# Filler products in TensorE's waits, and the mixer's small products in another order

## What is computed

```python
for l in range(DEPTH):          # 2
    h = rms_norm(x, norm_mix_g) * (1 + sc_m) + sh_m
    proj = h @ w_in             # neighbourhood, latent and grouped-query attention, 3 gates
    x = x + g_m * (merged @ w_out)
    h = rms_norm(x, norm_ffn_g) * (1 + sc_f) + sh_f
    x = x + g_f * ((silu(gate) * up) @ ffn_w_down)
x = rms_norm(x, final_norm_g)
```

```python
h = mixer(x, ...)               # branches y_lru, y_gdn, y_sb, y_gla, gated and merged
x = layer_norm(DN_ALPHA * x + h, ln1_g, ln1_b)
h = moe(x, w_router, router_bias, w_gate, w_up, w_down)
x = layer_norm(DN_ALPHA * x + h, ln2_g, ln2_b)
```

## Time and profile before

| what | value |
|---|---|
| median of 3 runs | 1788.84 us (1787.88 to 1794.1) |
| the profiled execution, its own time | 1784.76 us |
| its span | 1783.0 us |
| TensorE busy, share, records | 1584.5 us, 89%, 10701 |
| VectorE, ScalarE, GpSimd busy | 1224.1, 818.9, 43.5 us |
| mean clock granted to TensorE, of 2.4 GHz | 0.952 |
| transfers | 348.04 MB, mean 195 GB/s |

### The profile page before, as it was taken

The page is one execution under the profiler, slowest core; times in us unless marked ns, Lnnn a source line. Parts: engine busy times, 40 slices in busy tenths (PEclk is TensorE's granted clock), DMA queues, the critical chain, the costliest instruction groups (busy, mean ns, idle before and its releaser), DMA issues. The chain is left out here.

```text
span 1783.0 us, 25495 instructions
## 1 busy us (share of the span) xinstructions
PE 1584.5 (89%) x10701; PEld 1435.6 (81%) x10701; DVE 1224.1 (69%) x1352; ACT 818.9 (46%) x952; POOL 43.5 (2%) x60
## 2 busy tenths in 40 slices
PE   2799997999989999899969999787688979999995
PEld 2789987999888988799959898686677777888884
DVE  4877577888756648666545784633565868899895
ACT  1345543443334553434323465224453346777774
POOL 0100000000010000000000000000000000000000
PEclk9999999999989999999989999897897988999998
DMA  8974435999854324566536563111231546999993
GB/s 306 316 241 139 162 128 160 353 334 321 282 149 142 118 96 144 199 207 218 167 87 189 157 190 119 53 42 48 71 95 48 186 147 238 376 362 371 360 363 124
DMA packets 226055, 348.04 MB, mean 195 GB/s; under 512 B 14612, under 2 KB 156672, under 8 KB 225808
## 3 DMA queue, kind: packets, MB, share of 16 engines
q1 hardware_dynamic: 225936, 346.36, 58.2%
HBM read 345.29 MB, written 1.97 MB: 195 GB/s over the span
## 5 line engine op out<-in xcount | busy, mean ns | idle before, releaser
L459 PE MATMUL bank<-layer_split,hT_pair 128*128 128x256 f32 (+2 forms) x4032 | 512.9, 287 | 30.7 <-DVE hT_pair L1033 21.4
L459 PEld LDWEIGHTS bank<-layer_split,hT_pair 128*128 128x128 f32 x4032 | 486.6, 191 | 44.6 <-issue 29.3
L184 DVE TENSOR_TENSOR layer_split<-layer_raw,layer_split 128x2048 fp32r<-128x2048 f32 x122 | 279.6, 2292 | 100.5 <-ACT layer_split L172 98.9
L172 ACT ACTIVATE layer_split<-layer_raw 128x2048 fp32r<-128x2048 f32 x122 | 233.6, 1915 | 190.3 <-PE bank L459 73.0
L184 DVE TENSOR_TENSOR expert_split<-expert_raw,expert_split 128x2048 fp32r<-128x2048 f32 x96 | 219.0, 2289 | 26.4 <-ACT expert_split L172 25.9
L172 ACT ACTIVATE expert_split<-expert_raw 128x2048 fp32r<-128x2048 f32 x96 | 183.4, 1917 | 55.7 <-PE bank L2470 31.4
L459 PE MATMUL bank<-split_w,hT_pair 128*128 128x256 f32 (+1 forms) x1248 | 169.3, 297 | 13.7 <-PEq L2704 5.0
L459 PEld LDWEIGHTS bank<-split_w,hT_pair 128*128 128x128 f32 x1248 | 159.2, 196 | 24.1 <-issue 16.2
L184 DVE TENSOR_TENSOR split_w<-raw_w,split_w 128x2048 fp32r<-128x2048 f32 x52 | 119.2, 2292 | 63.6 <-ACT split_w L172 63.0
L1896 PE MATMUL bank<-layer_split,ffnh_aT 128*128 128x512 f32 x528 | 127.0, 396 | 2.8 <-DVE ffnh_aT L1964 2.8
L172 ACT ACTIVATE split_w<-raw_w 128x2048 fp32r<-128x2048 f32 x52 | 99.4, 1912 | 58.1 <-PE bank L459 49.7
(11 more groups left out here) (466 smaller groups left out, 1888.4 us busy)
## 6 DMA issues: line engine op xcount, KB each, us to landing
layer_raw<-in_ada_w SPq DMA_DIRECT2D x48, 1024.0 KB, 6.5
layer_raw<-in_ffn_w_gate_up SPq DMA_DIRECT2D x44, 1024.0 KB, 5.7
raw_w<-in_w_in SPq DMA_DIRECT2D x40, 1024.0 KB, 5.3
layer_raw<-in_w_in SPq DMA_DIRECT2D x38, 1024.0 KB, 6.4
expert_raw<-in_w_gate SPq DMA_DIRECT2D x32, 1024.0 KB, 7.2
expert_raw<-in_w_up SPq DMA_DIRECT2D x32, 1024.0 KB, 7.6
expert_raw<-in_w_down SPq DMA_DIRECT2D x32, 1024.0 KB, 7.3
layer_raw<-in_ffn_w_down SPq DMA_DIRECT2D x22, 1024.0 KB, 5.7
```

The source lines that it names most:

```text
L172: self.nc.scalar.activation(self.pair[:, j % self.pairs, 0, 0:self.size[n]], self.raw[:, n % self.depth, 0:self.size[n]], ACT.Copy).then_i ...
L184: self.nc.vector.tensor_tensor(self.pair[:, j % self.pairs, 1, 0:self.size[n]], self.raw[:, n % self.depth, 0:self.size[n]], self.pair[:, ...
L459: ins = nc.tensor.matmul(out, lhs, rhs, start=first and c == chunks[0] and tp + wp == 0, stop=last and c == chunks[-1] and tp == 1)
```

## The change

A helper issues n products of the table `ident` with 256 columns of the constants, in plain f32, into a bank that holds nothing at that time; the results are never read. `Beside` gets a method that does so in the bank of its next job, after the wait that this job would make. Calls are put in at 22 places, always ahead of a wait of TensorE or behind the last product ahead of one; by the number of times that each is run they issue 342 products. One call, at the end of layer 0's projection, has a new wait ahead of it (the bank of the job six from the end has been left). In `small_products` the 8 products of 256 columns move between the two tiles' products of 8 columns. The core of the diff:

```diff
+        def keep_busy(bank, n):
+            for _ in range(n):
+                nc.tensor.matmul(ps[bank][:, 0:256], ident, cst[:, 0:256], start=True, stop=True)
@@ class Norm, tensor
+                keep_busy(3, 14)
                 for t in range(TILES):
                     pe.wait_ge(self.normed.sem, t + 1)
                     self.turn.tensor_tile(t)
+                keep_busy(3, 14)
@@ class Beside
+            def keep_busy(self, pe, n):
+                g = self.issued
+                if g >= len(self.banks):
+                    pe.wait_ge(*self.jobs[g - len(self.banks)].left)
+                keep_busy(self.banks[g % len(self.banks)], n)
@@ class Projection, tensor
                     ada.reduce(pe, 1)
+                    keep_busy(3, 32)
                     pe.wait_ge(ring.acc_left, ada.done_pe)
                 else:
+                    keep_busy(2, 14)
                     norm.turn(pe, 0)
+                    keep_busy(2, 11)
...
                 self.ada_end = ada.done_pe
+                if self.l == 0:
+                    pe.wait_ge(*self.jobs[-6].left)
+                    keep_busy(len(self.jobs) % 6, 8)
@@ class FeedForward, tensor
                     if n >= 1:
                         down(n - 1)
+                    else:
+                        keep_busy(3, 12)
                     turn(n)
                 down(blocks - 1)
+                if self.norm_next is None:
+                    keep_busy(2, 10)
@@ routing, tensor, and routed_experts, tensor
+                keep_busy(7, 28)
                 for t in range(TILES):
                     pe.wait_ge(norm.normed.sem, t + 1)
...
+                keep_busy(7, 10)
                 pe.wait_ge(member_out.sem, 1)
...
                     route_tensor(pe)
+                    keep_busy(7, 10)
                     pe.wait_ge(g_ready, 1)
@@ small_products
                     for t in range(TILES):
                         for c in range(KD):
-                            nc.tensor.matmul(ps[7][:, 8 * t:8 * t + 8], hT[:, c, t * P:(t + 1) * P], small[:, c, 0:8],
+                            ins = nc.tensor.matmul(ps[7][:, 8 * t:8 * t + 8], hT[:, c, t * P:(t + 1) * P], small[:, c, 0:8],
+                                                   start=c == 0, stop=c == KD - 1)
+                        for c in range(KD if t == 0 else 0):
+                            nc.tensor.matmul(ps[7][0:16, S:2 * S], small[:, c, 8:24], hT[:, c, :],
                                              start=c == 0, stop=c == KD - 1)
-                    for c in range(KD):
-                        ins = nc.tensor.matmul(ps[7][0:16, S:2 * S], small[:, c, 8:24], hT[:, c, :],
-                                               start=c == 0, stop=c == KD - 1)
                     ins.then_inc(small_done, 1)
@@ lru_and_gdn, tensor
+                    beside.keep_busy(pe, 12)
                     pe.wait_ge(attn.sem, 2)
...
                         if n == 0:
+                            beside.keep_busy(pe, 28)
                             pe.wait_ge(started.sem, 4)
...
+                    beside.keep_busy(pe, 5)
                     pe.wait_ge(u_ready.sem, 10)
...
+                    beside.keep_busy(pe, 7)
                     pe.wait_ge(keyed.sem, 4)
...
+                    beside.keep_busy(pe, 9)
                     pe.wait_ge(squared.sem, 3)
...
                         nc.tensor.matmul(ps[b][:, :], ones, half(W(SQ), b), start=True, stop=True).then_inc(n_sum, 1)
+                    beside.keep_busy(pe, 14)
@@ stick_breaking, tensor
                             n = i - 1
+                            beside.keep_busy(pe, 28 if i == PAIRS else 8)
                             pe.wait_ge(kept.sem, 3 * n + 3)
@@ gla, tensor
-                for _ in range(5):
-                    yield
+                for i in range(5):
+                    if i == 3:
+                        keep_busy(4, 10)
+                    yield
+                beside.keep_busy(pe, 10)
                 pe.wait_ge(qk_ready.sem, 3)
...
+                beside.keep_busy(pe, 6)
                 pe.wait_ge(squared.sem, 1)
                 for b in range(2):
                     nc.tensor.matmul(ps[b][:, :], ones, half(bc_, b), start=True, stop=True).then_inc(n_sum, 1)
+                beside.keep_busy(pe, 14)
```

## The result

The change takes 1805.17 us (median of 7 runs, 1798.37 to 1813.53) beside 1788.29 us for the kernel before in the same session (7 runs, 1785.59 to 1794.1): a ratio of 1.0087, 95% interval 1.0068 to 1.0107. It is slower by 16.9 us; 10.7 were forecast. The profiled execution of the change was its slowest, 1813.53 us, and that of the kernel before among its fastest, 1784.76, so the two traces lie 28.7 us apart where the medians lie 16.9. I read sizes from the medians and places from the traces.

What follows compares the result with a forecast made beforehand. TensorE was taken to bound the kernel, with VectorE and ScalarE chains deciding its waits; filler lateness less clock returns summed to +10.7 us, 1795.5 by the profiled execution, forecast median 1799.5 us, range 1774 to 1812.

Steps and rivals of the forecast that it cites:

- The signs that it named: Fillers 0.216 us a record, inverse product five late, score at full clock, wide records 3.5 us, turn 5.1, clock above 0.98.
- The price: Each filler is two records 0.216 us apart: 0.43 us at 2.4 GHz, 0.85 at 1.2 GHz; 342 take 146 us.
- the rival with shorter fillers: Rival: at 0.27 us a filler every set ends within its wait and only returns remain, 1761.5 us; chance 0.14.
- Delta recurrence and stick products: 28 fillers outlast each wait: delta 5.4 late, 1.9 back, +3.4; last stick pair 5.9 late, 2.7 back, +3.0.
- Start of layer 0: 32 fillers end 4.9 us late, the next job 2.5 late; weight DMA has little in hand: +1.5, between 0 and +3.4.
- lateness hidden: Rival: slack in following stages (split weights, tanh, DMA) takes up half of 15.8 us of losses, median 1792; chance 0.28.
- End of projection: Layer 0: eight fillers (3.4 us) end at 108.5, 0.7 late, but the group and 72 records behind run faster: -2.2.
- Feed-forward, layer 0: Twelve fillers end 1.4 late; the 96 records behind shrink from 13.58 toward 11.14, the turn by 0.4: -1.2.
- Small products parted: Parting the 8-column rows keeps the clock, so 16 wide records take 3.5 us instead of 5.31: -1.8.
- Gated recurrence: Ten fillers in a 3.15 us wait: +0.9; at its end six and 14 more fillers: +1.0, 0 to +5.
- Routing: 28 fillers make scores 3.6 late; ten before counts hide but for 0.3; ten before the gather add 2.0: +2.7 overall.
- Fillers at half clock: Rival: sets after a block's end or small products start at 0.85 us a filler, 8 to 10 more, 1808; chance 0.13.

Runs made afterwards that it cites:

- run 6: Kernel before plus only the three sets of 28 fillers (delta recurrence, last stick-breaking pair, routing), at the change's lengths: 1800.47 us, 1.0051.
- run 4: The change with all its fillers but the small products in their old order: 1803.21 us, 1.0079.
- run 7: The change without the three filler sets right behind narrow products (8 at projection's end, 10 behind the router's, 6 behind the gated ones): 1805.62 us, 1.0092.
- run 3: The change with only its three sets of 28 fillers shortened, to 16, 13 and 16: 1793.94 us, 1.0024.
- run 9: Kernel before plus 89 fillers cut to their waits, only in layer 1's projection, the delta recurrence and the stick products: 1777.27 us, 0.9939.
- run 10: Kernel before plus 68 fillers cut to their waits: norms, feed-forward end, low-rank stage, gated merge and routing: 1789.1 us, 0.9998.
- run 1: The change with every filler set dropped, only the new order of the small products kept: 1791.49 us, 1.0027 against the kernel before.
- run 2: The change with its filler sets cut to the length of their waits, 198 products instead of 342: 1779.61 us, 0.9955.
- run 5: The change cut to 157 fillers: sets fitted to their waits, five sets without visible return dropped, small products in old order: 1778.99 us, 0.9941.
- run 11: The change with all 342 fillers in place, each of 128 columns instead of 256: 1781.4 us, 0.996.

## Why the prediction was right or wrong

The direction and the cause were right, and the measured 1805.17 lies in the range, 5.7 above the forecast and just above its own range of 1794 to 1805. The signs that it named are there: records 0.216 us apart, the inverse product 5.1 us behind its predecessor, the score at full clock (1.13 us for 2.04), the 16 wide records in 3.63, layer 1's turn 5.2 us behind the hidden products, a mean clock of 0.982.

Where it was off shows in one comparison. For the three sets of 28 the forecast had 3.4, 3.0 and 3.6 us, 10.0 together, and run 6 measured 10.7 by the medians. For everything else it had 0.7, and the medians leave 6.2: by the traces, the returns that it counted at the end of layer 0's projection, at that layer's feed-forward and at the parting, 5.2 us together, came in small part or not at all.

The steps against the traces, each as a stage's growth in us over the trace of before; the marks are starts of the same product in it:

| stage, up to (start before) | forecast | change | run 4 | run 7 | run 3 | run 6 | run 9 | run 10 | run 1, no sets |
|---|---|---|---|---|---|---|---|---|---|
| layer 0 (461.70) | -1.9 | +1.4 | -0.6 | -2.2 | +2.3 | -0.3 | +0.6 | -2.2 | -2.4 |
| attention, layer 1 (715.22) | +1.0 | +2.5 | +2.5 | +2.5 | +4.1 | +2.4 | -1.0 | +2.3 | +1.2 |
| feed-forward 1, final norm (981.19) | +2.3 | +3.4 | +3.6 | +3.6 | +3.4 | +0.1 | +2.2 | +0.6 | +0.3 |
| small products, next blocks (1089.95) | -1.8 | +1.6 | +1.0 | +1.9 | +0.7 | -0.6 | -1.0 | +1.2 | +0.7 |
| delta recurrence (1228.12) | +3.5 | +3.4 | +5.3 | +5.4 | -1.3 | +3.7 | -5.2 | +3.3 | +0.2 |
| stick products (1292.97) | +3.0 | +4.4 | +5.6 | +2.7 | -3.4 | +3.5 | -3.4 | -1.0 | -0.3 |
| gated recurrence (1401.55) | +1.9 | +5.1 | +2.0 | +2.0 | +1.6 | +3.3 | +0.2 | +2.9 | +6.5 |
| routing (1487.88) | +2.7 | +7.4 | +6.5 | +4.8 | +3.1 | +3.8 | -0.1 | 0.0 | 0.0 |

The traces of the change and of run 4 are those of their slowest executions, so their columns add up to about 29 and 26 us where the medians have 16.9 and 13.3; that of run 7 lies at its median. Run 10 has no filler in the delta recurrence and yet +3.3 there, run 1 none at all and +6.5 in the gated recurrence: a single entry is no size.

*The price*: right. 0.43 us a product was the first thing that the whole sum hung on; 56 records take 12.25 us, 12.0 were forecast. The Trainium skill, "TensorE: Matmul & The Clock Gate", Back-to-back issue gap, gives 109 ns for 256 columns; even with two records a product this is an estimate of 6.1 us for 28, inside their wait of 7.22. The trace of after decides for the rows, and the rival with shorter fillers falls with it.

*Delta recurrence and stick products*: right in mechanism and nearly in size. VectorE's last work for the first inverse product ends at 1133.5 (timeline of VectorE after):

```profile
1132.27 1.23 DVE L3326 TENSOR_TENSOR mixer_arena<-cst,mixer_arena 128x1024 f32<-128x1024 f32 x1
```

and the product starts at 1138.57, 5.1 us behind it; 5.4 were forecast. Run 6 gives +3.7 and +3.5 against +3.4 and +3.0. When the sets are cut, both stages turn to -5.2 and -3.4 (run 9; runs 2, 5 and 11 have -5.2, -3.7 and -5.4 in the first, so here the traces agree). In run 9's the return right behind the delta's set is 1.7 us (1.9 forecast) and behind the last pair 2.7 (2.7 forecast); the rest of the -5.2 comes at the stage's smaller sets, which no longer overrun. In the change the last pair's set took 1.8 us more than its price, part of it being at half clock.

*Start of layer 0*: the set ended as forecast, 5.2 us late (55.05 for 49.81, 4.9 forecast), and the lateness was gone by the projection's last block, where 0.6 is left (98.39; its predecessor's start in the trace of before is 97.8). The waits for split weights had it in hand, so here the rival *lateness hidden* had the case. The +1.5 is not seen, but kernels that are the same up to here start the block at 109.81 between 3.6 us earlier and 0.1 earlier, so neither value is shown.

*End of projection*: -2.2 forecast, about -0.4 in the trace. The step that failed is "eight fillers (3.4 us) end at 108.5": they stand behind 16 products of one column, at whose end (105.54) the clock fell, and took 5.36 us. The 72 records behind them were warm, as forecast, but started 2.1 late.

*Feed-forward, layer 0*: -1.2 forecast (its own terms, 1.4 - 2.4 - 0.4, give -1.4), +0.8 in the trace. The 96 records did shrink to 11.14 us. The next turn then waits 2.19 us for VectorE (the line at 321.05 above): TensorE had come back early to a wait that the slow clock had hidden. The return was counted without asking who was late next. In layer 1, where nothing could return, +2.3 was forecast, and 743.39 lies 2.2 further behind than the set's start did.

*Small products parted*: the -1.8 is wrong, by runs 1 and 4. Their products were sized right; the step that failed is "ScalarE and the whole next stage wait for the last", with nothing asked of the block behind, whose wait grew, whose first records took the low clock over, and which already pauses for split weights in the trace of before (run 1). The clock did not fall "during the long row of small ones" either, but at 984.99, just behind it.

*Gated recurrence*: +0.9 and, at the end, 0 to +5; together they hold the 5.1, but with run 1's +6.5 beside it no size can be taken from one trace.

*Routing*: +2.7 forecast, +7.4 and +6.5 found, the largest miss; +4.8 in run 7, without the ten before the counts. The 28 are worth +3.8 (run 6), 3.6 were forecast. "Ten before the counts hide behind a VectorE split but for 0.3" failed: the router's products of 16 columns took 4.96 us instead of 3.73, the ten behind them 6.66 instead of 4.3. In run 7 the counts are as late beside the trace of before as the router's products (20.5 us); in the change 26.4 us at the router's products became 31.7 at the counts.

*Fillers at half clock*, 1808: near the measured time, and partly by luck. It named the start, the 14 after the final sums, the 28 in routing and the 20 at the final norm. Of these only the start ran slow (16.74 us for 13.8); the 14 take 6.21 us (1393.77) and the 28 take 12.32, full clock. The slow ones stood elsewhere, three of them behind narrow products. Against the 148 us of 684 records 0.216 apart, the page's 163.5 are 15 more: 4.6 of it is the overlap named above, and about 11 is half clock, of which the part in waits is free.

*Lateness hidden*, 1792, fell: half of the losses should have been taken up, and in the change's trace every stage adds to the lateness behind the first layer and none takes from it; run 6's 10.7 for a sum of 10.0 says the same by medians.

The prediction also said that at most half of 171 us of low clock, less what is idle, could come back. The Trainium skill, "TensorE: Matmul & The Clock Gate", Terms, puts the penalty at the throttled time times (1 - K/N): an estimate of 86 us by that rule. The trace disagrees with the rule as a forecast of a gain: of the 170.0 us of low clock in its record 69.6 found TensorE idle, where a clock costs nothing, and half of the other 100.4 is 50. The change, with the clock at 0.982, got 38.5 us back by the page's account, 33.9 by the starts.

What stays open: how much of the last 6 us of the change's 16.9 belongs to which set outside the three; two traces of one instruction stream differ by as much. That a set behind narrow products is worse than one elsewhere was tried (run 7) and not found in the time.

## What to carry to other kernels

Work that is only there to keep the clock up is worth its place until shortly before the wait ends, and past the end it costs its full length: here nearly the same places gained 0.45% with sets that fit their waits (run 2) and lost 0.9% with 1.7 times as many fillers. Take its price from the spacing of a row of the same form, not from its time in flight; leave a microsecond of each wait open, since the products behind it were as warm where 1.2 to 1.8 us stayed open; put it only in front of work that is on the path and cold now, and ask what that work waits for when it comes early. And measure by medians of many runs: a clock that falls here or there by chance moves one trace of this kernel by 6 us.

## What the runs showed of the hardware that I had not expected

- The clock fell while TensorE was busy without a pause, or with one of 0.19 us, in or right behind narrow products: behind 5.59 us of 160-column records and 16 of one column, the fillers from 105.58 took 0.335 us a record instead of 0.219; the router's 32 records of 16 columns, with the same 28 wide products in front, took 4.96 us in the change and 3.71 in run 7. It fell in both, 2.2 us behind their first record in the change and 4.6 us in run 7, when they were done: what the fall costs depends on where it lands.
- Filling a wait does not raise the clock for good: a cold stretch of about the same length turned up a little further on when one was cured (run 1, run 7).
- Products half as wide hold the clock too: in run 11 the same 684 records, 90.5 us in all, brought it to 0.975 and gave back 23.8 us of other work (1584.5 - 1560.7), where the change's 163.5 us brought 0.982 and 38.5.
